# A decoder trunk on eight cores: adaLN modulation tiles placed in the attention loop, and one matmul fewer per full score pair

## The reference

```
def trunk(x, c, ...):
    for i in range(DEPTH):                                  # 2 layers
        mod = silu(c) @ w_mod[i] + b_mod[i]                 # adaLN: 6 x 1024 columns a layer
        sh1, sc1, g1, sh2, sc2, g2 = split(mod, 6)
        h = rms_norm(x, g_mix[i]) * (1 + sc1) + sh1
        if i == 0:  out = dilated_mixture(h, w_qkv, w_o, rel_bias, bufs)
        else:       out = conformer_conv(h, ...)
        x = x + g1 * out
        h = rms_norm(x, g_ffn[i]) * (1 + sc2) + sh2
        x = x + g2 * (silu(h @ w_gate[i]) * (h @ w_up[i])) @ w_down[i]
    return rms_norm(x, g_final), new_attn, new_conv
```

## Time and profile before

| | us |
|---|---|
| median of the 2 runs | 4244.55 (4200.19 and 4288.91) |
| the profiled execution | 4193.87 |
| its span on the slowest core | 4192.3 (cores 4166.2 to 4192.3) |
| TensorE busy | 2890.2 (69%) |
| VectorE busy | 1432.6 (34%) |
| ScalarE busy | 994.2 (24%) |
| first stage, up to the barrier at L418 | 248.8 |
| attention, up to the barrier at L636 | 248.8 to 1849.6 |

### The profile page before, as it was taken

The page is one execution under the profiler, slowest core; times in us unless marked ns, Lnnn a source line. Parts: engine busy times, 40 slices in busy tenths (PEclk is TensorE's granted clock), DMA queues, the critical chain, the costliest instruction groups (busy, mean ns, idle before and its releaser), DMA issues.

```text
span 4192.3 us, 58740 instructions; the slowest of 8 cores (4166.2 to 4192.3 us)
## 1 busy us (share of the span) xinstructions
PE 2890.2 (69%) x21070; PEld 1534.1 (37%) x21070; DVE 1432.6 (34%) x2770; ACT 994.2 (24%) x2198; POOL 392.7 (9%) x354
## 2 busy tenths in 40 slices
PE   1258777778787786845437999918357773599991
PEld 0135344444454444534214554404123331244440
DVE  2324454545444545354241211121203235121213
ACT  2432222222222121211022101031064743310100
POOL 0100000000000000013031001040000002210103
PEclk9668677777786777755678999969678896799995
DMA  9941010111111101039504446304930000454632
GB/s 172 193 69 43 13 43 17 41 24 33 24 33 25 39 18 39 21 65 165 130 0 61 65 63 80 66 8 48 21 25 1 1 1 1 50 76 69 74 66 81
DMA packets 228349, 216.44 MB, mean 52 GB/s; under 512 B 46176, under 2 KB 188128, under 8 KB 227040
## 3 DMA queue, kind: packets, MB, share of 16 engines
q0 software_dynamic: 157232, 146.85, 24.3%
q1 hardware_dynamic: 70832, 65.83, 8.6%
HBM read 326.53 MB, written 32.96 MB: 86 GB/s over the span
## 4 chain that ended last, share of the span: by engine, by line
PE 55%; DVE 14%; DMA 8%; ACT 8%; issue 7%; POOL 4%; another core or an unknown queue 2%; DVEq 1%; ACTq 0%; POOLq 0%; SPq 0%
PE ps_b L278 55%; DMA wst<-w_mod 5%; POOL tmp L291 4%; ACT dg L288 4%; DVE Pb L291 3%; DVE rDs L617 3%; DVE Nacc L291 3%; ACT hF L288 2%; DMA Kc<-ck 1%; DMA wo_sb<-w_o 1%; DVE Dsl L291 1%; DVE sq L291 1%; DVEq L134 1%; ACT rstd L288 1%
## 5 line engine op out<-in xcount | busy, mean ns | idle before, releaser
L278 PE MATMUL ps_b<-hT,wq 128*128 128x512 bf16 (+3 forms) x2752 | 495.6, 344 | 21.0 <-DMA wq<-wqkv 21.0
L278 PE MATMUL ps_b<-hF,wg 128*128 128x512 bf16 (+2 forms) x1936 | 364.6, 328 | 128.0 <-DMA wg<-w_gate 128.0
L278 PE MATMUL ps_b<-hF,wu 128*128 128x512 bf16 (+2 forms) x1936 | 362.4, 327 | 0.0
L278 PE MATMUL ps_b<-Pb,Vb 128*128 128x128 bf16 (+2 forms) x976 | 179.1, 271 | 238.1 <-DVE Pb L291 122.6
L278 PEld LDWEIGHTS ps_b<-hT,wq 128*128 128x128 bf16 x2752 | 239.2, 104 | 280.2 <-issue 73.4
L278 PE MATMUL ps_b<-aT,wd 128*128 128x512 bf16 (+2 forms) x1936 | 323.2, 326 | 4.8 <-DVE aT L291 4.8
L291 DVE TENSOR_TENSOR aT<-gsb,ps_b 128x512 bf16<-128x512 f32 (+1 forms) x242 | 135.0, 558 | 530.0 <-PE ps_b L278 508.1
L278 PE MATMUL ps_b<-uT,dg 128*128 128x512 bf16 x992 | 224.2, 388 | 126.0 <-ACT dg L288 126.0
L288 ACT ACTIVATE gsb<-ps_b 128x512 f32<-128x512 f32 (+1 forms) x242 | 119.3, 493 | 691.9 <-PE ps_b L278 691.2
L278 PE MATMUL ps_b<-wq,hT 128*128 128x128 bf16 x4736 | 282.9, 222 | 0.0
L278 PEld LDWEIGHTS ps_b<-wq,hT 128*128 128x128 bf16 x4736 | 279.7, 125 | 0.0
(11 more groups left out here) (154 smaller groups left out, 2982.3 us busy)
## 6 DMA issues: line engine op xcount, KB each, us to landing
wst<-w_mod POOLq DMA_DIRECT2D x24, 1024.0 KB, 18.1
wg<-w_gate POOLq DMA_DIRECT2D x44, 512.0 KB, 6.9
wu<-w_up POOLq DMA_DIRECT2D x44, 512.0 KB, 8.7
wd<-w_down POOLq DMA_DIRECT2D x32, 704.0 KB, 7.1
wq<-wqkv POOLq DMA_DIRECT2D x24, 768.0 KB, 6.9
xstage<-xT SPq DMA_DIRECT2D x8, 2048.0 KB, 21.2
Kc<-ck POOLq DMA_DIRECT2D x48, 256.0 KB, 8.0
Vc<-ck POOLq DMA_DIRECT2D x48, 256.0 KB, 6.7
```

Source lines behind the costliest of these rows:

```text
L278: ins = pe.matmul(out_ap, l, r, start=(i == 0), stop=(i == n - 1))
```

## The change

Three things are changed.

First, the 20 tiles of `rest_tiles` leave the first stage. They become 40 tiles of 256 columns, and two of them are made at the head of each of the first 20 attention units, after `load_unit` of the next unit and before Q. They have two buffers of their own (`wsu`, in the part of memory that attention uses). The bfloat16 copy of the conditioning vectors, `csb`, moves so that it stays alive. The three `scale_cols` stand behind the last unit.

Second, the four score matmuls of a full pair become three. The middle block of keys is used by its own queries and by those of the block after it, which lie side by side, so the two products with it become one of 256 columns.

Third, `rDs` goes, to make room: the reciprocal is written over `Dsl`.

```diff
-        def mod_tile(l, ft):
+        def mod_tile(l, ft, width=512, bufs=None, bname="wst"):
+            bufs = bufs or wst
             wv = w_mod[l].rearrange("(k p) f -> p k f", p=128)
             s = modit[0] % 2
             modit[0] += 1
-            dma("pool", wst[s][:], wv[:, :, ft * 512:(ft + 1) * 512], (), (f"wst{s}",))
+            nfc = width // 128
+            dma("pool", bufs[s][:, :, :width], wv[:, :, ft * width:(ft + 1) * width], (), (f"{bname}{s}",))
             pb, pbn = mmbank()
...
-        rest_tiles = [(0, ft) for ft in range(4, 12)] + [(1, ft) for ft in range(12)]
+        rest_tiles = [(0, ft) for ft in range(8, 24)] + [(1, ft) for ft in range(24)]
...
             norm_prompt(xstage[s][:], (f"xstage{s}",), hT[:, :, t0:t0 + 512], (f"hT{tt}",), 512, 0, 0, 0, "dve")
-            for _ in range(3 if tt < 4 else 2):
-                if rest_tiles:
-                    mod_tile(*rest_tiles.pop(0))
-        while rest_tiles:
-            mod_tile(*rest_tiles.pop(0))
         dma("sp", xstage[0][:, :, :NS], xsT, (), ("xstage0",))
         norm_sample(xstage[0][:, :, :NS], ("xstage0",), hT[:, :, SEQ:SEQ + NS], ("hTs",), 0, 0, 0)
-        scale_cols(0, 1)
-        scale_cols(1, 0)
-        scale_cols(1, 1)
...
-        rDs = hi.alloc("rDs", [1, 2176], F32)
+        wst2 = [hi.alloc(f"wsu{i}", [128, KC, 256], BF16) for i in range(2)]
...
             if ui + 1 < len(units):
                 load_unit(ui + 1)
+            for _ in range(2):
+                if rest_tiles:
+                    mod_tile(*rest_tiles.pop(0), width=256, bufs=wst2, bname="wsu")
...
+                if full_pair:
+                    res, a = lay[0][0][0], lay[0][0][1]
+                    mm_group(S[:, 0:128], [(KTv[:, res, (a - 1) * 128:a * 128], QTv[:, res, a * 128:(a + 1) * 128])],
+                             ("KT", "QT"), (Sn,))
+                    mm_group(S[:, 128:384], [(KTv[:, res, a * 128:(a + 1) * 128], QTv[:, res, a * 128:(a + 2) * 128])],
+                             ("KT", "QT"), (Sn,))
+                    mm_group(S[:, 384:512], [(KTv[:, res, (a + 1) * 128:(a + 2) * 128],
+                                              QTv[:, res, (a + 1) * 128:(a + 2) * 128])], ("KT", "QT"), (Sn,))
...
-                    P.add("dve", lambda e: e.reciprocal(rDs[:], Dsl[:]), ("Dsl",), ("rDs",))
+                    P.add("dve", lambda e: e.reciprocal(Dsl[:], Dsl[:]), ("Dsl",), ("Dsl",))
...
+        while rest_tiles:
+            mod_tile(*rest_tiles.pop(0), width=256, bufs=wst2, bname="wsu")
+        scale_cols(0, 1)
+        scale_cols(1, 0)
+        scale_cols(1, 1)
```

More of the change, by code:

```diff
@@ L315, in build @@
         m_hiA = hi.mark()
+        csb = hi.alloc("csb", [128, KC, 1 + NS], BF16)
         hT = hi.alloc("hT", [128, KC, SEQ + NS], BF16)
@@ L318, in build @@
         wst = [lo.alloc(f"wst{i}", [128, KC, 512], BF16) for i in range(2)]
-        csb = lo.alloc("csb", [128, KC, 1 + NS], BF16)
         P.add("dve", lambda e: e.tensor_copy(csb[:], csT[:]), ("csT",), ("csb",))
@@ L329, in mod_tile @@
             modit[0] += 1
-            dma("pool", wst[s][:], wv[:, :, ft * 512:(ft + 1) * 512], (), (f"wst{s}",))
+            nfc = width // 128
+            dma("pool", bufs[s][:, :, :width], wv[:, :, ft * width:(ft + 1) * width], (), (f"{bname}{s}",))
             pb, pbn = mmbank()
[L332 to L336, removed]
+            for fc in range(nfc):
+                pairs = [(bufs[s][:, k, fc * 128:(fc + 1) * 128], csb[:, k, :]) for k in range(KC)]
+                mm_group(pb[:, fc * 32:fc * 32 + 1 + NS], pairs, (f"{bname}{s}", "csb"), (pbn,))
+            for fc in range(nfc):
+                j = ft * nfc + fc
                 act(modT[:, l, j, :], pb[:, fc * 32:fc * 32 + 1 + NS], AF.Identity, (pbn, "vec"), (mres(l, j),),
@@ L565, in stage1 @@
                     qcol += n
[L566 to L570, removed]
+                full_pair = (len(lay) == 2 and all(l_[0][2] == 0 and l_[0][3] == 0 for l_ in lay))
+                if full_pair:
[6 more added lines that the diff above has]
+                                              QTv[:, res, (a + 1) * 128:(a + 2) * 128])], ("KT", "QT"), (Sn,))
+                else:
+                    for (res, a, i0, et), subs, n, qc in lay:
+                        for (kind, ka, sc) in subs:
+                            mm_group(S[:, sc:sc + n],
+                                     [(KTv[:, res, ka * 128:(ka + 1) * 128], QTv[:, res, a * 128 + i0:a * 128 + 128])],
+                                     ("KT", "QT"), (Sn,))
                 act(Pf[sb_][:, :col], S[:, :col], AF.Exp, (Sn,), (f"Pf{sb_}",))
-                full_pair = (len(lay) == 2 and all(l_[0][2] == 0 and l_[0][3] == 0 for l_ in lay))
                 if full_pair:
@@ L616, in do_norm @@
                 def do_norm(slot=slot):
-                    P.add("dve", lambda e: e.reciprocal(rDs[:], Dsl[:]), ("Dsl",), ("rDs",))
+                    P.add("dve", lambda e: e.reciprocal(Dsl[:], Dsl[:]), ("Dsl",), ("Dsl",))
                     for (c0, n) in pieces(0, 2176):
                         pb, pbn = mmbank()
-                        mm_group(pb[:, :n], [(ones_f[0:1, :], rDs[0:1, c0:c0 + n])], ("ones_f", "rDs"), (pbn,))
+                        mm_group(pb[:, :n], [(ones_f[0:1, :], Dsl[0:1, c0:c0 + n])], ("ones_f", "Dsl"), (pbn,))
                         dve_tt(OT[:, slot, c0:c0 + n], Nacc[:, c0:c0 + n], pb[:, :n], ALU.mult, ("Nacc", pbn),
```

## The result

The changed kernel takes 0.9929 of the time before, with a 95% interval of 0.9915 to 0.9944. Its profiled execution took 4161.0 us (before: 4193.9), its cores 4142.2 to 4159.4 us. A second measurement on another occasion gave 0.9937 (0.9912 to 0.9963). I had forecast a sum of -40.9 us; the profiled executions differ by 32.9 us, and 0.71% of 4194 us is 30 us. The medians over all executions are 4174.77 us after and 4247.62 us before, and they are not compared here, nor with the forecast: executions of either kernel in which some cores have a lower clock lie in both, in different numbers.

The account below looks back on a forecast made before the run. Bytes were taken to bound the first 249 us, with the norm chain next. Terms -3.6 - 61.7 - 5.4 + 3.1 + 10.7 + 15 + 2 - 1 = -40.9 us from 4193.9 gave 4153, stated as 4155; range 4125 to 4198.

Parts of the forecast that it names:

- case A: Whole kernel: all terms add up as summed, 4155 us, with bounds of some 4135 to 4172; chance 0.74.
- point 1: First stage: without the moved loads the norms bind at 14.3 us each; start 3.6 us sooner, norms gain 61.7 us.
- point 3: Unit 0: its matmuls wait for two modulation tiles loaded behind two `wq`; cost +10.7 us, bounds 9.5 to 13.
- The tail: First stage's end: `rstd` follows `hT` at once, 2.4 us to the barrier, gain 5.4; `scale_cols` returns after attention, +3.1 us.
- point 5: Unit heads: 640 small modulation matmuls cost 20 us at 31 ns, partly offset at the lower clock; taken 15, bounds 10 and 20.
- Later units: Units after 0: `wq` and two tiles load in 12.8 us, hidden under at least 18.8 us; cost 0.
- 5 and 6: Unit heads: small modulation matmuls, +15 us, and ScalarE's evacuations delaying a bank, +2 us (bounds 0 and 6).
- The merge: Score groups: 88 pairs use three matmuls for four, but columns bind; -1 us, bounds 0 and -5.
- The in-place reciprocal: Attention's `Dsl`: later writes already stand behind the same broadcast matmuls; cost 0, else 7 times some tenths.
- a sign of being wrong: Attention stretch: growth of more than 30 us was named as showing the prediction wrong.

Follow-up runs that it names:

- run from unit 1 on: Changed kernel with the moved modulation tiles at the heads of units 1 to 20 instead of 0 to 19; ratio to before 0.9896 (0.9881 to 0.9910).
- run before V: Changed kernel with each unit's two moved tiles between its K and V matmuls instead of at its head; ratio to before 0.9926 (0.9901 to 0.9951).

## Why the prediction was right or wrong

The mechanism held: bytes bound the first stage, the norm chain took over, unit 0 waits, no later unit does, the merge is nothing. What the profiles show is case A. The size did not hold. The sum had 40.9 us; the profiled executions give 32.9, and the two ratios 30 and 26, so 8 to 15 are missing.

The step that failed is the term for the first stage, point 1 and above all its first part, the earlier start of the norms. The stage's gain was put at 70.7 us (3.6 + 61.7 + 5.4) and measured 65.0; the start was to give 3.6 of them and gave nothing. The other missing part lies in the stages behind attention, which the sum put at nothing and which were 9.9 us longer in the changed kernel's two profiles (2342.7) than in the four with the long first stage (2332.7); its cause stays open.

By its own points:

1. First stage. Means over the cores, of four profiles with the long form and of the two of the changed kernel (differences taken before rounding):

| part | forecast | measured |
|---|---|---|
| start of the first square | -3.6 | +0.5 (53.0 to 53.5) |
| from there to the end of the last `hT` | -61.7 | -60.2 (182.0 to 121.9) |
| from there to the barrier | -5.4 | -5.3 (7.7 to 2.4) |
| together | -70.7 | -65.0 (242.8 to 177.8) |

The start is 4.1 of the 5.7 us. I had seen that the fourth load took 12.4 us for 7.3 us of bytes, and put the rest down to the later loads behind it in the queue. They went, and the fourth load still takes as long: 11.4 us from its issue to its first matmul, 11.3 before. Here it is on core 2 of after, from the chain of waits, and two windows over it (busy times of five engines, granted clock, DMA share, GB/s):

```profile
39.93 11.78 DMA wst<-w_mod
...
39.90:43.00 3.10, 0.00 (x0) 0.00 (x0) 0.00 (x0) 0.77 (x3) 0.87 (x1) 1.00 0.35 54
43.00:50.30 7.30, 1.01 (x32) 0.94 (x32) 0.00 (x0) 1.10 (x4) 0.00 (x0) 1.00 1.07 143
```

From 41 to 51 us only the software queue moved data, but for 0.02 MB of instructions, so no x load of this core was a neighbour either. The bytes take 7.3 us as reckoned; the other 4 us are mostly before them, with the DMA engines little used. They belong to the load and not to a neighbour on this core, and unit 0's loads have some such time too (point 3).

The 1.5 us of the second part came from taking the profiled core, whose eight norms took 184.7 us, for all of them. The same core hid the error of the start: its first square stood at 56.38, 3.4 us behind the mean, and 3.6 taken from that is close to the mean's 53.5. So that the barrier came where I said (178.1; 178.3 and 177.2 in the means) is in part luck. The differences between cores stood in front of me: their spans differed by 26 us.

2. The tail: on core 2 hT to barrier 179.77 - 177.37 = 2.4 us, as forecast, and `scale_cols` 2.9 for 3.1.

3. Unit 0: +10.7 forecast. On core 2 of both profiles the first Q matmul moved from 10.0 to 23.1 us behind the barrier, 13.1, of which 1.0 is the matmuls that I counted in point 5, so 12.1. It was inside my bounds (9.5 to 13). The run from unit 1 on gives 9.0 to 10.9 for it. The second tile landed 2.1 us after the first had begun to be used at 20.0; the rate of 144 GB/s held, and my sum had left out the time that a load takes beside its bytes, some 2 us here (22.6 us for the second tile to be ready, 20.5 forecast). By the Trainium skill's rate for such loads (DMA: Bandwidth & Descriptors, Anatomy of one DMA), bytes over 436 GB/s, my estimate for the two tiles would have been 5 us less; the trace shows 144 GB/s at a DMA share of 0.97 with all eight cores loading and casting.

4. Later units: cost 0 was right, for a wait; the run from unit 1 on shows that unit 1 is covered too.

5 and 6. Matmuls and banks: 15 + 2 = 17 us forecast for 20 units, 16.5 measured in the run from unit 1 on. The size was right, with two errors in it that work against each other. The small matmuls hold TensorE 0.87 us a unit, 17.4 us and not 20: 31 ns is the mean busy time of one, and they start 27 ns apart. And I had the slow stretch at a unit's head last as long as before; it lasted 0.4 to 0.5 us longer from the first matmul, so that Q runs 0.4 us less at the lower clock. At half the rate that gives back 0.2 us a unit, 4 us in all (an estimate), where I had taken 5. That leaves 13.4 us, and 3 for the banks and whatever else I don't see.

7. The merge: -1 forecast, +1 measured (interval -4 to +6 us). My 107 ns a matmul is 128 columns at 1.2 GHz; the row has 0.40 us for four, 100 ns each. The in-place reciprocal costs nothing that shows: TensorE's eight waits for it sum to 116.2 us in both.

Attention in all: +29.8 forecast, +29.4 measured in the means (30.9 by the first profiles, just over the 30 that I had named as a sign of being wrong, and 27.8 by the two taken side by side later). The two touched stages thus leave 35.6 us. The second ratio's interval reaches from 16 to 37 us, the first from 23 to 36, so both hold the 35.6 or nearly. From 40.9 to 35.6 it is the first stage; from there to 26, the difference of the mean spans (4173.4 and 4147.7), it is the untouched stages.

The time itself, 4155 us, was 6 us below the profiled execution, which lies within the range. It was made against one execution of 4193.9, while the others that the first ratio compares reach up to 4206.

## What to carry to other kernels

When a stage is relieved of its bytes, compute what binds next before celebrating, and see whether that can be overlapped too: here the chain that took over was worth more than what the change had gained. Put moved work where an engine already waits for something else, not at the head of a loop that it bounds: the same tiles cost 27 us at the heads of units and 5 beside the reciprocals, and leaving out the first iteration alone gave 9 to 11. Before counting on a load to come sooner when its neighbours go, find out how much of its time is its own beside the bytes: here it was 4 of 11.4 us, and the neighbours were worth nothing. Subtract stages by their mean over cores and over more than one execution, for the slowest core's own stage can be a biased sample: here it was 248.8 us, and the mean 242.8.

## What the hardware showed that I had not expected

- Matmuls of 17 columns with a new 128 x 128 weight each start 27 ns apart at the lower clock (32 in the 0.87 us up to the next matmul, at a granted clock of 0.50) and 25 ns apart at the upper one (32 in 0.81 us in unit 0 of the run before V, at 1.00). So the clock hardly matters to them, and at the lower one they cost about a quarter of what a score matmul of 128 columns costs (100 ns).
- Three matmuls of 128, 256 and 128 columns took the same 0.40 us as four of 128.
- The fourth cast load, 1.05 MB, took 11.3 us from its issue to its first matmul with another load behind it and 11.4 us with none. About 7.3 us of that moved its bytes.
- Two more groups in the rotation of banks, behind a store of K that ScalarE waits for, cost TensorE 6.5 us of waits over attention.
- The stage with a 1.9 MB store from SBUF (the conformer's gated projection) varied from 224 to 240 us between executions of kernels that are the same there: on the profiled core the store landed in 91.0 us before and 89.5 us after, and on cores 0, 2, 5 and 7 in 84 to 91 us in these two profiles and in 70 to 87 in the nine later ones.
